# One more round of lag in the attention pipeline of a two-block fp32 kernel, with a third buffer for the probabilities

## The chip, the cores and the metric

The kernel runs on one NeuronCore of a Trainium2 chip. The metric is the device time of one execution in microseconds (us); lower is better. TensorE is called PE in the profile (PEld is its weight-load side), VectorE DVE, ScalarE ACT, GpSimd POOL and SyncE SP.

## What is computed

A sequence of 512 tokens of width 1024 goes through two layers of a first block and then two layers of a second block, all in float32. The parts of the reference that matter here are its attentions, each a masked softmax of scores times values, in blocks of 128 queries:

```python
def one_block(args):
    q_blk, blk = args
    s = jnp.einsum('bqhmd,bkhmd->bhmqk', q_blk, k).astype(jnp.float32) * scale
    ...
    s = jnp.where(mask, s, -jnp.inf)
    p = jax.nn.softmax(s, axis=-1).astype(v.dtype)
    return jnp.einsum('bhmqk,bkhd->bqhmd', p, v)
...
# first block, per layer
y_mem = memory_cross_attention(xq, mem_n, ...) @ w_cross_o[l]      # 4 heads, 256 memory rows
y_diff = diff_attention(dq, dk, dv, ...) @ w_diff_o[l]             # 8 heads, two maps each
y_mla = latent_attention(c_q, c_kv_kr, ...) @ w_mla_o[l]           # 8 heads of 96
merged = gates[:, :, 0] * y_diff + gates[:, :, 1] * y_mla + gates[:, :, 2] * y_mem
x = x + merged @ w_out[l]
# second block, per layer: dsa_mixer and nsa_mixer (4 heads each), a short convolution, a pooling
```

The second block's attentions are over compressed keys (31 of them), over selected and windowed keys, and over the top 128 keys of an index score.

## The kernel before, in words

Every engine has its own program, written out by hand in order, and they meet at counting semaphores. Projections (`project`, L377 and L379) take each weight slab of 128 rows through a ring of four slabs (SP issues the loads), POOL splits it into a high and a low part (L292, L295), and PE multiplies three combinations of parts, 12 matmuls of 512 columns a slab.

Attention is cut into units: one unit is a block of 128 queries for two heads (or the two maps of a head), with n keys. A unit takes six steps:

- `scores` (PE, L525, mask L530) into one of two pairs of PSUM banks (`u % 2`);
- `maximum` (DVE, L567);
- `exp` (ACT, L581) into one of two slots of `probs` (`u % 2`), with the row sums;
- `turn` (PE, L544, L546), the transposes of the probabilities into the one pair of banks 4 and 5;
- `copy` (ACT, L593) out of them into one of two slots of `probs_t`;
- `weight` (PE, L557), the products with the values, and `finish` (DVE, L1150 to L1167 and L1658 to L1677), the scaling by the row sums.

`attend` puts the PE steps into rounds: round i has scores of unit i, turn of unit i - 2, weight of unit i - 3, in this order. `steps` does the same for ACT (copy of i - 2, then exp of i) and DVE (maximum of i, finish of i - 3, and a piece of other work where `between` has one). Scores of unit i wait for exp of unit i - 2, since they share banks. There are 88 units a pass over both blocks: cross (8 units, n = 256), diff (32 units) and mla (16 units) in each layer of block one, and 32 in each layer of block two. In diff and mla the key counts follow one another as 128, 512, 256, 384.

Where attend has a `projection`, the rounds behind the last scores (the tail) are set in front of slabs 1, 2, ... of the next projection: `lat0` behind cross, `gate00` behind mla. Diff and block two have nothing between the tail's rounds. After the mla attention DVE squares and sums the diff outputs (L1248, L1250), scales them (L1254) and signals `outs_ready`, for which PE waits in front of the transposes `o_t0` and `o_t1` (L391); these follow `gate00`, and behind them stands the projection `gate01`.

Of the kernel before, what the change touches and what calls it, by code (L numbers as in the profile page):

```python
# [28 lines left out]
P = 128  # L29
# [3 lines left out]
W512 = 512  # L33
# [52 lines left out]
def program(nc, io, out):  # L86
    ctx = ExitStack()
    with ctx:
# [6 lines left out]
        m = {}  # L95
        for name, floats in (("arena", 80 * 256), ("outs", 32 * 256)):
# [9 lines left out]
            "probs": sb("probs", [P, 2, 2, W512]),  # L106
# [7 lines left out]
            "small": sb("small", [P, 2304]),  # L114
# [120 lines left out]
class Layer:  # L235
# [87 lines left out]
    def attend(self, pe, A, lo, hi, before_turns=None, projection=None):  # L323

        ahead, first = 0, self.done[-1 if len(self.done) % 2 else -2]
        if before_turns:
            ahead = 2  # L330

            def scores():
                self.emptied(pe, first)
                A.scores(lo)
                A.scores(lo + 1)

            self.project(pe, *before_turns, {4: scores})
        else:
            self.emptied(pe, first)
        parts = [(0, A.scores), (2, A.turn), (3, A.weight)]  # L340
        for i in range(lo, hi + 1):
            A.round(i, lo, hi, parts, ahead)
            if i == lo:
                self.emptied(pe, self.done[-1])
        for name in self.order.names[len(self.done):][:2]:
            self.first_wait[name] = (self.s["finished" if self.order.index(name) % 2 else "exped"], hi)
        tail = [lambda i=i: A.round(i, lo, hi, parts) for i in (hi + 1, hi + 2)]
        if projection:
            self.project(pe, *projection, {1 + k: f for k, f in enumerate(tail)})
        else:  # L350
            for f in tail:
                f()
# [140 lines left out]
class Attention:  # L493
# [39 lines left out]
    def turn(self, u):  # L533
        pe, a = self.nc.tensor, self.units[u]
        pe.wait_ge(self.s["exped"], u + 1)
        if u >= 1:
            pe.wait_ge(self.s["turned_copied"], u)
        for j in range(2):
            for kb in range(0, a["n"], P):
                src = self.m["probs"][:, u % 2, j, kb:min(kb + P, a["n"])]  # L540
                width = src.shape[1]
                dst = self.m["ps"][0:width, 4 + j, kb:kb + P]
                if width == P:
                    last = pe.transpose(dst, src, self.m["ident"][:])  # L544
                else:
                    last = pe.matmul(dst, src, self.m["ident"][:], start=True, stop=True)  # L546
        last.then_inc(self.s["turned"], 1)
# [27 lines left out]
    def exp(self, u):  # L575
        act, a = self.nc.scalar, self.units[u]
        act.wait_ge(self.s["maxed"], u + 1)
        if u >= 2:
            act.wait_ge(self.s["turned"], u - 1)
        for j in range(2):  # L580
            last = act.activation(self.m["probs"][:, u % 2, j, 0:a["n"]],  # L581
# [46 lines left out]
def block_one(nc, io, m, s, layer):  # L628
# [68 lines left out]
    gated, merging = (m[n][:].rearrange("p a b n -> p (a b) n") for n in ("probs", "probs_t"))  # L697
# [84 lines left out]
    with nc.Block() as block:  # L782
# [100 lines left out]
        def _(act):  # L883
# [82 lines left out]
            A.steps(0, U1, (2, A.copy), (0, A.exp), ahead=2)  # L966
# [20 lines left out]
            A.steps(U1, U2, (2, A.copy), (0, A.exp), between={prep_rounds[-2]: lambda: roots(st_both)})  # L987
# [4 lines left out]
            A.steps(U2, U3, (2, A.copy), (0, A.exp))  # L992
# [38 lines left out]
        def _(dve):  # L1031
# [139 lines left out]
            A.steps(0, U1, (0, A.maximum), (3, finish), ahead=2)  # L1171
# [69 lines left out]
            A.steps(U1, U2, (0, A.maximum), (3, finish), between=dict(zip(prep_rounds, pieces)))  # L1241
            A.steps(U2, U3, (0, A.maximum), (3, finish))
# [62 lines left out]
def block_two(nc, io, m, s, layer):  # L1305
# [67 lines left out]
    U = len(units)  # L1373
# [17 lines left out]
    with nc.Block() as block:  # L1391
# [70 lines left out]
        def _(act):  # L1462
# [57 lines left out]
            A.steps(0, U, (2, A.copy), (0, A.exp))  # L1520
# [3 lines left out]
        def _(dve):  # L1524
# [155 lines left out]
            A.steps(0, U, (0, A.maximum), (3, finish), between={2 + k: lambda k=k: piece(k) for k in range(len(ops))})  # L1680
# [9 lines left out]
            fresh = m["probs"][:].rearrange("p a b n -> p (a b) n")  # L1690
# [94 lines left out]
```

## Time and profile before

| what | value |
|---|---|
| median of 3 runs | 2975.85 us (2973.08 to 2976.11) |
| the profiled execution: time, span of its instructions | 2971.55 us, 2969.7 us |
| PE busy, share of the span | 2740.5 us, 92% |
| DVE, ACT, POOL busy | 1081.9, 746.6, 1868.5 us |
| mean granted clock of PE | 0.967 |

The busy time of PE has modelled ends, so a full row of PE means that it had work all along and not that it ran at its peak. The granted clock is 1.00 at 2.4 GHz and 0.50 at 1.2 GHz.

### The profile page before, as it was taken

Reading aid. Unit: us, or ns where it says so; the run is one execution under the profiler, and the core shown is the slowest. Engines: PE = TensorE matmul, PEld = TensorE weight load, DVE = VectorE, ACT = ScalarE, POOL = GpSimd, SP = SyncE. Lnnn points to the kernel's source line nnn. Section 1 sums busy time; section 2 is a strip of 40 time slices with the busy share of each in tenths; the row PEclk is TensorE's granted clock in tenths of the full one; section 3 lists DMA queues with packets and bytes.
Section 4 is the critical chain, followed back from the end, with each engine's and each line's share of the span. In section 5 each row is a group of like instructions: output and inputs, shape, how many; then the busy total and the mean of one; then the engine's idle time right before and its main releaser. Section 6 shows DMA issues by size and latency. Waiting matters only on the chain. (4 is left out here: it accounts for less than half of the span.)

```text
span 2969.7 us, 38883 instructions
## 1 busy us (share of the span) xinstructions
PE 2740.5 (92%) x14264; PEld 2252.2 (76%) x14268; DVE 1081.9 (36%) x1902; ACT 746.6 (25%) x1455; POOL 1868.5 (63%) x1562
## 2 busy tenths in 40 slices
PE   6898999999999997899999999999998998989997
PEld 4687777778888886678777778888887976778765
DVE  4354364211210113245183320310102486427773
ACT  3241464200220201331365110120111114212250
POOL 5547321788898995647420788898896772366604
PEclk9999999999999998999999999999998999999998
DMA  4322100233233333322100233223233430042202
GB/s 123 85 61 77 41 8 12 81 93 96 89 96 97 95 96 81 96 77 74 52 8 1 72 88 96 90 93 99 93 99 79 94 79 29 29 89 76 76 1 71
DMA packets 159285, 214.80 MB, mean 72 GB/s; under 512 B 51696, under 2 KB 69360, under 8 KB 159088
## 3 DMA queue, kind: packets, MB, share of 16 engines
q1 hardware_dynamic: 120336, 207.27, 24.1%
q10 hardware_dynamic: 38752, 4.95, 1.3%
q8 instruction: 118, 1.93, 0.3%
q14 instruction: 79, 0.65, 0.1%
HBM read 210.06 MB, written 2.10 MB: 71 GB/s over the span
## 5 line engine op out<-in xcount | busy, mean ns | idle before, releaser
L292 POOL TENSOR_TENSOR weight_parts<-weight_ring,zero 128x512 fp32r<-128x512 f32 (+3 forms) x736 | 791.2, 1075 | 775.8 <-PE ps L377 396.9
L295 POOL TENSOR_TENSOR weight_parts<-weight_ring,weight_parts 128x512 fp32r<-128x512 f32 (+4 forms) x804 | 1062.1, 1321 | 155.3 <-ACT weight_parts L303 97.0
L379 PE MATMUL ps<-h_feature_major_high,weight_parts 128*128 128x512 f32 x2304 | 584.8, 394 | 13.1 <-ACT arena L1486 5.3
L379 PEld LDWEIGHTS ps<-h_feature_major_high,weight_parts 128*128 128x128 f32 x2304 | 431.0, 189 | 117.1 <-POOL weight_parts L292 10.0
L377 PE MATMUL ps<-weight_parts,h_feature_major_high 128*128 128x512 f32 (+3 forms) x1920 | 438.7, 369 | 39.1 <-DVE h_feature_major_low L1687 9.1
L377 PEld LDWEIGHTS ps<-weight_parts,h_feature_major_high 128*128 128x128 f32 x1920 | 344.3, 193 | 94.4 <-issue 18.8
L379 PE MATMUL ps<-h_feature_major_low,weight_parts 128*128 128x512 f32 x1152 | 310.0, 391 | 0.0
L377 PE MATMUL ps<-weight_parts,ut_high 128*128 128x512 f32 x1024 | 254.7, 390 | 0.0
L379 PEld LDWEIGHTS ps<-h_feature_major_low,weight_parts 128*128 128x128 f32 x1152 | 217.5, 189 | 45.8
L377 PE MATMUL ps<-weight_parts,h_feature_major_low 128*128 128x512 f32 (+3 forms) x960 | 234.7, 368 | 0.0
L377 PEld LDWEIGHTS ps<-weight_parts,ut_high 128*128 128x128 f32 x1024 | 191.6, 188 | 42.2 <-POOL weight_parts L295 1.7
L567 DVE TENSOR_REDUCE negmax<-ps 128x2 f32<-128x512 f32 (+4 forms) x176 | 132.7, 754 | 240.1 <-ACT arena L985 113.9
L557 PE MATMUL ps<-arena,probs_key_major 128*128 128x128 f32 (+1 forms) x1632 | 216.4, 279 | 0.0
L525 PE MATMUL ps<-arena 64*128 64x512 f32 (+9 forms) x704 | 169.7, 480 | 42.5 <-ACT probs L581 23.8
L557 PEld LDWEIGHTS ps<-arena,probs_key_major 128*128 128x128 f32 (+1 forms) x1632 | 198.5, 194 | 6.5 <-issue 6.0
L581 ACT ACTIVATE probs<-ps,negmax 128x256 f32<-128x256 f32 (+4 forms) x352 | 172.7, 499 | 97.7 <-DVE negmax L567 87.1
L377 PEld LDWEIGHTS ps<-weight_parts,h_feature_major_low 128*128 128x128 f32 x960 | 176.0, 194 | 24.1
L1295 DVE TENSOR_TENSOR ut_low<-outs,ut_high 128x2048 fp32r<-128x2048 f32 x16 | 45.1, 2816 | 319.6 <-ACT ut_high L1027 319.6
L593 ACT ACTIVATE probs_key_major<-ps 128x512 f32<-128x512 f32 (+4 forms) x176 | 116.6, 662 | 122.5 <-PE ps L544 113.9
L1023 ACT ACTIVATE outs<-ps 128x2048 f32<-128x2048 f32 x16 | 30.1, 1883 | 429.7 <-PE ps L379 429.7
L377 PE MATMUL ps<-weight_parts,ut_low 128*128 128x512 f32 x512 | 136.9, 390 | 0.0
L525 PEld LDWEIGHTS ps<-arena 64*128 64x128 f32 (+2 forms) x704 | 76.9, 200 | 73.5 <-ACT probs L581 33.1
(245 smaller groups left out, 2848.8 us busy)
## 6 DMA issues: line engine op xcount, KB each, us to landing
weight_ring<-in_w_in SPq DMA_DIRECT2D x272, 256.0 KB, 2.7
weight_ring<-in_w_mlp SPq DMA_DIRECT2D x256, 256.0 KB, 2.7
weight_ring<-in_w_out SPq DMA_DIRECT2D x64, 256.0 KB, 2.6
weight_ring<-in_w_mem_kv SPq DMA_DIRECT2D x32, 256.0 KB, 2.9
weight_ring<-in_w_diff_o SPq DMA_DIRECT2D x32, 256.0 KB, 2.6
weight_ring<-in_w_in SPq DMA_DIRECT2D x32, 170.0 KB, 2.7
weight_ring<-in_w_in SPq DMA_DIRECT2D x32, 168.0 KB, 2.2
weight_ring<-in_w_in SPq DMA_DIRECT2D x32, 163.0 KB, 2.2
```

Source lines behind the costliest of these rows:

```text
L292: self.nc.gpsimd.tensor_tensor(high, raw, self.m["zero"][:].broadcast_to([P, raw.shape[1]]), ALU.add).then_inc(self.s["slab_high"], 1)
L295: self.nc.gpsimd.tensor_tensor(low, raw, high.bitcast(F32), ALU.subtract).then_inc(self.s["slab_split"], 1)
L377: last = self.nc.tensor.matmul(banks[:, t, 0:width], h[:, cut], w, **ends)
L379: last = self.nc.tensor.matmul(banks[:, t, :], w[:, cut], h, **ends)
L525: last = pe.matmul(bank[:, 0:a["n"]], a["q"][j], a["k"][j], start=True, stop=a["mask"] is None)
L557: last = pe.matmul(self.m["ps"][:, 6 + u % 2, j * P:(j + 1) * P], self.m["probs_t"][0:rows, u % 2, j, kb * P:(kb + 1) * P], a["v"][j](kb), ...
L567: last = dve.tensor_reduce(out, self.m["ps"][:, 2 * (u % 2):2 * (u % 2) + 2, 0:a["n"]], AX.X, ALU.max, negate=True)
L581: last = act.activation(self.m["probs"][:, u % 2, j, 0:a["n"]], self.m["ps"][:, 2 * (u % 2) + j, 0:a["n"]], ACT.Exp, bias=self.m["negmax"] ...
L593: act.activation(self.m["probs_t"][0:rows, u % 2, :, 0:width], self.m["ps"][0:rows, 4:6, 0:width], ACT.Copy).then_inc(self.s["turned_copie ...
L1023: a.activation(r, L.banks(f"up{f}{j}"), ACT.Relu)
L1295: v.tensor_tensor(ut[1][:, 4 * j:4 * j + 4, :], rect[(f * ups + j) % 2], ut[0][:, 4 * j:4 * j + 4, :].bitcast(F32), ALU.subtract).then_inc ...
```

## The change

The transposes move from two to three rounds behind the scores, the value products and the finish from three to four, and `probs` gets a third slot, so that exp of unit u waits for the transposes of unit u - 3 instead of u - 2. The tail of each attend has one more round. The scratch `small` is shortened from 2304 to 2128 floats to make room. The PSUM banks of the scores stay two pairs, and `probs_t` keeps two slots.

```diff
-            "probs": sb("probs", [P, 2, 2, W512]),
+            "probs": sb("probs", [P, 3, 2, W512]),
...
-            "small": sb("small", [P, 2304]),
+            "small": sb("small", [P, 2128]),
...
-        parts = [(0, A.scores), (2, A.turn), (3, A.weight)]
+        parts = [(0, A.scores), (3, A.turn), (4, A.weight)]
...
-        tail = [lambda i=i: A.round(i, lo, hi, parts) for i in (hi + 1, hi + 2)]
+        tail = [lambda i=i: A.round(i, lo, hi, parts) for i in (hi + 1, hi + 2, hi + 3)]
...
-                src = self.m["probs"][:, u % 2, j, kb:min(kb + P, a["n"])]
+                src = self.m["probs"][:, u % 3, j, kb:min(kb + P, a["n"])]
...
         act.wait_ge(self.s["maxed"], u + 1)
-        if u >= 2:
-            act.wait_ge(self.s["turned"], u - 1)
+        if u >= 3:
+            act.wait_ge(self.s["turned"], u - 2)
         for j in range(2):
-            last = act.activation(self.m["probs"][:, u % 2, j, 0:a["n"]],
+            last = act.activation(self.m["probs"][:, u % 3, j, 0:a["n"]],
...
-            A.steps(0, U1, (2, A.copy), (0, A.exp), ahead=2)
+            A.steps(0, U1, (3, A.copy), (0, A.exp), ahead=2)
...
-            A.steps(0, U1, (0, A.maximum), (3, finish), ahead=2)
+            A.steps(0, U1, (0, A.maximum), (4, finish), ahead=2)
...
```

The other calls of `steps` change in the same way, and three views of `probs` as scratch take its first two slots.

On PE, at the start of the diff attention (first layer), the rounds of units 3 to 5 stood so (L525 and L530 scores and mask, L544 transposes, L557 value products):

```order
246 L525 MATMUL ps<-arena 128x384 x2
247 L530 MATMUL ps<-causal,ident 128x128 x2
248 L544 MATMUL ps<-ident,probs 128x128 x8
249 L557 MATMUL ps<-arena,probs_key_major 128x128 x2
250 L525 MATMUL ps<-arena 128x128 x2
251 L530 MATMUL ps<-causal,ident 128x128 x2
252 L544 MATMUL ps<-ident,probs 128x128 x4
253 L557 MATMUL ps<-arena,probs_key_major 128x128 x8
254 L525 MATMUL ps<-arena 128x512 x2
255 L530 MATMUL ps<-causal,ident 128x128 x2
256 L544 MATMUL ps<-ident,probs 128x128 x6
257 L557 MATMUL ps<-arena,probs_key_major 128x128 x4
```

The same rounds in the changed kernel:

```order
245 L525 MATMUL ps<-arena 128x384 x2
246 L530 MATMUL ps<-causal,ident 128x128 x2
247 L544 MATMUL ps<-ident,probs 128x128 x2
248 L525 MATMUL ps<-arena 128x128 x2
249 L530 MATMUL ps<-causal,ident 128x128 x2
250 L544 MATMUL ps<-ident,probs 128x128 x8
251 L557 MATMUL ps<-arena,probs_key_major 128x128 x2
252 L525 MATMUL ps<-arena 128x512 x2
253 L530 MATMUL ps<-causal,ident 128x128 x2
254 L544 MATMUL ps<-ident,probs 128x128 x4
255 L557 MATMUL ps<-arena,probs_key_major 128x128 x8
```

The transposes of each unit stand one round later and so behind the scores of another unit: the 4 transposes of a 256-key unit stood behind the short scores of a 128-key unit, and stand now behind the long ones of a 512-key unit.

On PE, where the mla attention ends and `gate00` begins (L379), the order was:

```order
427 L557 MATMUL ps<-arena,probs_key_major 128x128 x8
428 L379 MATMUL ps<-h_feature_major_high,weight_parts 128x512 x4
429 L379 MATMUL ps<-h_feature_major_low,weight_parts 128x512 x4
430 L379 MATMUL ps<-h_feature_major_high,weight_parts 128x512 x4
431 L544 MATMUL ps<-ident,probs 128x128 x6
432 L557 MATMUL ps<-arena,probs_key_major 128x128 x4
433 L379 MATMUL ps<-h_feature_major_high,weight_parts 128x512 x4
434 L379 MATMUL ps<-h_feature_major_low,weight_parts 128x512 x4
435 L379 MATMUL ps<-h_feature_major_high,weight_parts 128x512 x4
436 L557 MATMUL ps<-arena,probs_key_major 128x128 x6
```

In the changed kernel the same place reads, from the end of slab 0 on:

```order
429 L544 MATMUL ps<-ident,probs 128x128 x4
430 L557 MATMUL ps<-arena,probs_key_major 128x128 x8
431 L379 MATMUL ps<-h_feature_major_high,weight_parts 128x512 x4
432 L379 MATMUL ps<-h_feature_major_low,weight_parts 128x512 x4
433 L379 MATMUL ps<-h_feature_major_high,weight_parts 128x512 x4
434 L544 MATMUL ps<-ident,probs 128x128 x6
435 L557 MATMUL ps<-arena,probs_key_major 128x128 x4
436 L379 MATMUL ps<-h_feature_major_high,weight_parts 128x512 x4
437 L379 MATMUL ps<-h_feature_major_low,weight_parts 128x512 x4
438 L379 MATMUL ps<-h_feature_major_high,weight_parts 128x512 x4
439 L557 MATMUL ps<-arena,probs_key_major 128x128 x6
```

The last value products stood behind two slabs of `gate00` and now stand behind three, and one more unit's transposes and value products moved from in front of `gate00` into it.

## Rows read from the trace of the kernel before

**Rows 1.** The page: span, and busy time of the engines
```profile
span 2969.7 us, 38883 instructions
...
PE 2740.5 (92%) x14264; PEld 2252.2 (76%) x14268; DVE 1081.9 (36%) x1902; ACT 746.6 (25%) x1455; POOL 1868.5 (63%) x1562
```

**Rows 2.** Instructions of line 544 (turn): what its engine's idle time waited for
```profile
  ACT probs_key_major L593: 8.3, 21
  ACT probs L581: 1.6, 2
```

**Rows 3.** Instructions of line 557 (weight): what its engine's idle time waited for
```profile
  ACT probs_key_major L593: 0.4, 2
```

**Rows 4.** The waits: who waited for whom, total us, times, longest us
```profile
PEld ps L525 <- ACT probs L581: 33.1, 44, 1.5
```

**Rows 5.** Windows: stretch, us, each engine busy (instructions), PEclk granted, DMA share, GB/s
```profile
336.00:432.00 96.00, 86.19 (x659) 65.25 (x659) 73.00 (x169) 60.85 (x172) 16.02 (x12) 0.98 0.03 7
448.00:500.00 52.00, 48.57 (x308) 38.04 (x307) 21.24 (x55) 28.86 (x83) 0.00 (x0) 0.90 0.00 1
451.60:461.60 10.00, 9.66 (x30) 6.10 (x28) 2.87 (x3) 2.81 (x10) 0.00 (x0) 0.50 0.00 0
...
528.30:532.00 3.70, 3.66 (x32) 3.42 (x32) 1.03 (x2) 1.75 (x4) 3.54 (x4) 1.00 0.10 11
1662.00:1665.90 3.90, 3.89 (x24) 3.90 (x25) 0.55 (x1) 1.27 (x3) 3.74 (x4) 0.65 0.13 16
2480.00:2535.00 55.00, 49.75 (x379) 36.76 (x378) 47.36 (x125) 30.63 (x98) 0.00 (x0) 1.00 0.01 1
```

**Rows 6.** Timeline (start us, us, engine, line, op, [idle before]): DVE, block two
```profile
2497.21 0.15 DVE L1662 RECIPROCAL recip<-rowsum 128x2 f32<-128x2 f32 x1
...
2498.41 1.22 DVE L1626 TENSOR_TENSOR arena<-arena,small 64x1024 f32<-64x1024 f32 x1
```

**Rows 7.** Timeline, end of mla, gate00 and the transposes behind it, first layer
```profile
498.10 0.63 PE L544 MATMUL ps<-ident,probs 128*128 128x128 f32 x4 [0.76 <-ACT probs_key_major L593]
...
500.27 1.17 PE L379 MATMUL ps<-h_feature_major_high,weight_parts 128*128 128x512 f32 x4
...
507.41 1.50 PE L557 MATMUL ps<-arena,probs_key_major 128*128 128x128 f32 x12
...
512.40 1.07 PE L379 MATMUL ps<-h_feature_major_low,weight_parts 128*128 128x512 f32 x4
...
515.12 1.07 PE L379 MATMUL ps<-h_feature_major_low,weight_parts 128*128 128x512 f32 x4
...
528.25 3.71 PE L391 MATMUL ps<-ident,outs 128*128 128x128 f32 x32 [2.63 <-DVE outs L1254]
...
533.80 1.17 PE L379 MATMUL ps<-h_feature_major_high,weight_parts 128*128 128x512 f32 x4 [1.84 <-issue]
```

**Rows 8.** Timeline, PE at the same place in the second layer
```profile
1662.01 5.38 PE L391 MATMUL ps<-ident,outs 128*128 128x128 f32 x32 [2.63 <-DVE outs L1254]
1668.18 1.16 PE L379 MATMUL ps<-h_feature_major_high,weight_parts 128*128 128x512 f32 x4 [0.80 <-issue]
```

**Rows 9.** Timeline, DVE between cross attention and its work on the latent
```profile
250.66 0.77 DVE L1047 SCALAR_TENSOR_TENSOR outs<-arena 128x384 f32<-128x384 f32 x1 [17.09 <-ACT arena L910]
```

**Rows 10.** Timeline of PE, in the diff attention of the first layer
```profile
382.92 0.63 PE L544 MATMUL ps<-ident,probs 128*128 128x128 f32 x4 [0.30 <-ACT probs_key_major L593]
383.28 1.87 PEld L557 LDWEIGHTS ps<-arena,probs_key_major 128*128 128x128 f32 x16
...
386.04 1.13 PE L525 MATMUL ps<-arena 64*128 64x512 f32 x4 [0.71 <-ACT probs L581]
...
392.68 0.86 PEld L544 LDWEIGHTS ps<-ident,probs 128*128 128x128 f32 x8
```

**Rows 11.** Timeline, PE at the end of block two's attention, first layer
```profile
2555.11 1.07 PE L544 MATMUL ps<-ident,probs 128*128 128x128 f32 x8 [0.63 <-ACT probs_key_major L593]
```

More of the change, by code:

```diff
@@ L696, in block_one @@
     gates = [view(arena, 16384 + 2048 * k, 4, SEQ) for k in range(2)]
-    gated, merging = (m[n][:].rearrange("p a b n -> p (a b) n") for n in ("probs", "probs_t"))
+    gated, merging = (m[n][:, 0:2].rearrange("p a b n -> p (a b) n") for n in ("probs", "probs_t"))
     od = view(outs, 0, TT, D)
@@ L986, in _ @@
                 last.then_inc(emptied, 1)
-            A.steps(U1, U2, (2, A.copy), (0, A.exp), between={prep_rounds[-2]: lambda: roots(st_both)})
+            A.steps(U1, U2, (3, A.copy), (0, A.exp), between={prep_rounds[-2]: lambda: roots(st_both)})
             for k in range(2):
@@ L991, in _ @@
                 scaled(f"m_t{2 + k}", [(kmt[0:MQK, 4 * k + h, :], h, MQK, SEQ, mkg[0:MQK]) for h in range(4)])
-            A.steps(U2, U3, (2, A.copy), (0, A.exp))
+            A.steps(U2, U3, (3, A.copy), (0, A.exp))
             roots(st_o)
@@ L1240, in _ @@
             L.emptied(dve, "kvb1")
-            A.steps(U1, U2, (0, A.maximum), (3, finish), between=dict(zip(prep_rounds, pieces)))
-            A.steps(U2, U3, (0, A.maximum), (3, finish))
+            A.steps(U1, U2, (0, A.maximum), (4, finish), between=dict(zip(prep_rounds, pieces)))
+            A.steps(U2, U3, (0, A.maximum), (4, finish))
             v.drain()
@@ L1519, in _ @@
             empty("cmp_t", [(kcmpt, L.banks("cmp_t")[:, 0, 0:NCMP], ACT.Copy, 1.0)])
-            A.steps(0, U, (2, A.copy), (0, A.exp))
+            A.steps(0, U, (3, A.copy), (0, A.exp))
             L.square_right(act, 1, junk)
@@ L1678, in finish @@
                 last.then_inc(s["finished"], 1)
-            A.steps(0, U, (0, A.maximum), (3, finish), between={2 + k: lambda k=k: piece(k) for k in range(len(ops))})
+            A.steps(0, U, (0, A.maximum), (4, finish), between={2 + k: lambda k=k: piece(k) for k in range(len(ops))})
             def mix_in(src, at, chunks):
@@ L1689, in _ @@
             full(dve, "mix_t")
-            fresh = m["probs"][:].rearrange("p a b n -> p (a b) n")
+            fresh = m["probs"][:, 0:2].rearrange("p a b n -> p (a b) n")
             v.tensor_tensor(fresh, L.banks("mix_t"), fm[:, 0:4, :], ALU.mult)
```

## The prediction

> **What bounds the kernel now.** I read the page first. PE is busy for 2740.5 of 2969.7 us [rows 1], so the kernel is bound by PE's work and by the places where PE stands idle. The change adds and removes no matmul, so it can act only on idle time and on the clock. Next I read the waits for the pairs that the lag touches. A later turn can relieve two of them: turn waiting for its own unit's exp, 1.6 us in 2 instances [rows 2], and weight waiting for the copy, 0.4 us in 2 [rows 3]. The whole relief it is made for is 2.0 us of 2970. The large wait is another: scores wait 33.1 us, 44 times, for the exp of the unit two before, because the scores have two pairs of banks [rows 4]. That distance stays two, and the third slot of probabilities gives them no bank. The slot itself is only what the longer lag needs: exp would otherwise wait for transposes that stand a round later.
>
> Then I read the stages by windows [rows 5]. In diff PE has 86.19 busy us of 96, in mla 48.57 of 52: mostly bound by PE, where idle can hardly shrink. In block two's attention, from 2480 to 2535, DVE is busy for 47.36 of 55 us and its steps follow one another (the finish of a unit runs from 2497.21 until other work begins at 2498.41 [rows 6]): bound by DVE. The total of DVE's work does not change either.
>
> Last I read what stands behind the attention. In mla's layer PE finishes `gate00` and then waits 2.63 us for the scaled outputs, in both layers [rows 7, 8]. So the DVE chain from the last finish to `outs_ready` is not hidden now. Whatever delays the last value products delays the kernel.
>
> **The change part by part.** All terms are for one layer; there are two of each.
>
> *Cross.* Its tail lies in `lat0` and grows by one slab. Key counts are all equal, so nothing is re-paired. DVE ends later by about a slab, but it stands idle for 17.09 us between its work on the queries and keys and the latent's [rows 9], so this costs nothing; without that cover it would be a slab, up to 2.7 us.
>
> *Diff.* One gain and one loss. The gain: once in four rounds, the transposes of a 256-key unit wait some 0.3 us for the copy of a 512-key unit (382.92 [rows 10]); 8.3 us in 21 instances over the kernel [rows 2]. Now the scores of a 512-key unit, 1.13 us instead of a 128-key unit's, stand between them, so that wait goes: at most 7 times 0.3 = 2.1 us. The loss: while PE waits for exp (0.71 at 386.04 [rows 10]), it has done less than before, by one unit's transposes and value products. After the last such wait PE is the bound and owes that unit. For the largest unit this is 0.86 + 1.87 = 2.7 us [rows 10]; for the mean unit, with 2.5 blocks of keys against 4, 1.7 us. The first rounds also have one less turn to fill the wait for the first exps. Between -2.1 and +2.7, neither end nearer by any row, I take a little above the middle: +0.5.
>
> *mla and the outputs.* Before `gate00` the last transposes wait 0.76 us for the copy of the 512-key unit [rows 7]. They move into `gate00` behind a slab and this wait goes: -0.7. The last value products now stand behind three slabs instead of two. One slab takes 2.72 us (512.40 to 515.12 [rows 7]). From the value products at 507.41 to the transposes at 528.25 DVE's chain takes 20.8 us and I leave it as it is. So `outs_ready` comes 2.7 - 0.7 = 2.0 us later, while PE arrives 0.7 earlier: its wait grows from 2.63 to about 5.3 us, and the kernel loses +2.0. Bounds: 1.3 (two waits of 0.7 saved) to 2.7 (none).
>
> *Block two.* One unit's finish, 1.2 us (2497.21 to 2498.41 [rows 6]), leaves the stretch that DVE bounds and falls behind it, where DVE has time: -1.2. The turn's wait for its exp stands at this stage's start, half of the 1.6 us a layer [rows 2]: -0.8. The tail has one more round in which transposes and copy take turns, where a single wait was 0.63 [rows 11]: +0.4. Sum -1.6, bounds -2.0 and +0.6 (only the tail's loss).
>
> *The clock.* The same wait of 2.63 us leaves the clock at 1.00 in the first layer and brings it to 0.65 on the mean in the second, where the transposes take 5.38 instead of 3.71 us [rows 5, 7, 8]. A wait of 5.3 us should bring it down in both. What is behind needs the first 16 of the 32 transposes: half of 3.71, 1.85 us, at half the clock 1.85 more; I take 1.6 in the first layer. In the second layer `gate01` starts 6.17 us after the transposes begin against 5.55 in the first, so 0.6 is paid already; the clock falling earlier adds 0.7. Together +2.3 for both layers, between 0 and 3.1. The Trainium skill, TensorE: Matmul & The Clock Gate, "Why this matters for your kernels", says to leave no longer idle gaps between bursts of matmuls, as the clock falls to half after them. [...]
>
> **Sum.** 2 x (0 + 0.5 + 2.0 - 1.6) + 2.3 = +4.1 us. Against the profiled execution, 2971.55, this is 2975.7; that run lies 4.3 us below the median of the runs, so against the median 2975.85 I predict 2980. This is 0.14% slower. A difference of 0.2%, 6 us, is about what can be told from no change here.
>
> **The rivals.**
>
> *Half the clock lasts longer (slower).* At mla's start PE runs 10 us at 0.50, busy for 9.66 of them [rows 5], and block two has a like stretch. With one round more of scores alone, PE's work there is thinner. If each of the four stretches is a third longer, 3.4 us, half is lost: 4 x 1.7 = 6.8. With the forecast's 4.1 this is +11, 2987. It decides from about 2 us of loss on. Against it: a change of the mix could as well end the stretches sooner. The Trainium skill, the same page, "Part 4: PE-mode transpose", says that transposes do not count as busy for the clock. By that the 32 transposes behind the longer wait would not bring it back, and `gate01` would start slow as well. In the second layer the mean clock over the transposes is 0.65 and not 0.50 throughout [rows 5], which is no proof either way.
>
> *No change.* The re-pairing gives all of its gain (diff -2.1, block two -2.0) and the outputs' delay is 2.0: 2 x (-2.1 + 2.0 - 2.0) + 0 to 2.3 = -4.2 to -1.9, about 2973. Speaks for it: each bound is a row; against: the debt of one unit in diff.
>
> *Faster.* The lag changes how ACT's rounds are filled. In blocks of 128 keys, copy plus exp were 3, 7, 3, 7 in four rounds and are now 5, 6, 5, 4; PE's rounds go from 7, 9, 6, 8 to 6, 10, 7, 7. Evener rounds on ACT could let exp come sooner, and the 33.1 us of waits [rows 4] shrink. The losses above are 2 x 2.0 + 2.3 = 6.3 us, so it needs 12.3 us of 33.1 to be told as faster; with half, -16.5, it gives 2966. Against it: in block two, and in diff's first rounds, exp waits for a maximum that DVE's other work holds up (DVE busy 47.36 of 55 and 73.00 of 96 us [rows 5]), not for ACT.
>
> **How the numbers follow.** Forecast +4.1, own range 0 to +8 (2976 to 2984): 0.52, of which 0.14 lies above +6. Longer half clock: 0.18. No change: 0.18. Faster: 0.12. So faster 0.12, same 0.38 + 0.18 = 0.56, slower 0.14 + 0.18 = 0.32. The range that leaves out 2 in 10 reaches from 2969, between the faster case and no change, to 2988, just above the longer half clock.
>
> **What would show it.** In the trace after: turn's wait for exp gone, and few waits of L544 for L593 between the rounds; the waits of L525 for L581 still at some 30 us or more; the wait of the transposes L391 for L1254 at about 5 us in both layers, and the clock below 1.00 behind it in both; diff's stage as long as before within 2 us; block two's attention 1 to 2 us shorter. I am wrong if L525's waits fall by a third or more, if the wait for `outs_ready` stays near 2.6, or if the stretches at 0.50 change in length.

## The result, and the profile after

| | kernel before | changed kernel |
|---|---|---|
| median, beside each other on one chip | 2974.80 us (2969.24 to 2980.51, 20 runs) | 2983.08 us (2975.43 to 2990.96, 20 runs) |
| ratio, 95% interval | | 1.0026 [1.0018, 1.0034] |
| span of the profiled execution | 2969.7 us | 2981.4 us |
| mean granted clock of PE | 0.967 | 0.962 |

The changed kernel is 0.26% slower, about 7.7 us. The time lies in the forecast's range (2969 to 2988) and 3 us above its value of 2980. Taken as a difference, the growth of 7.7 us is nearly twice the forecast +4.1; that the two times lie closer comes from the median of the kernel before, which is 1 us lower here than the one that the forecast started from. Of the three cases I had held "within 0.2%" the likeliest; it became "slower", with the lower end of its interval (1.0018) just short of that line. Block two's term came out with the wrong sign, and those of mla and diff at another size. Line numbers of the changed kernel are those of before. In the experiments they are 1 to 7 higher, so L544 of the profile can be L545 or L548 there.

The page of the changed kernel answers to [rows 1]: no work was added, and PE is still busy for 92%.
```profile
span 2981.4 us, 38883 instructions
...
PE 2748.3 (92%) x14268; PEld 2261.8 (76%) x14268; DVE 1086.7 (36%) x1902; ACT 751.8 (25%) x1455; POOL 1870.4 (63%) x1562
```

The waits of the changed kernel, who waited for whom with the total, the times and the longest, answer to [rows 4]:
```profile
PEld ps L525 <- ACT probs L581: 31.8, 34, 2.2
```
The sum of the scores' waits stayed (33.1 before), but they are 34 in place of 44 and the longest has grown from 1.5 to 2.2 us. What L544 waits for answers to [rows 2]:
```profile
  ACT probs_key_major L593: 5.3, 8
  ACT probs L581: 1.3, 2
```
The waits for the copy fell from 21 to 8, by 3.0 us, and the two for exp hardly moved (1.6 to 1.3). One of these two stands here, first in the kernel before and then in the changed one; the other is at the same place of the second layer:
```profile
2555.08 0.86 PEld L544 LDWEIGHTS ps<-ident,probs 128*128 128x128 f32 x8 [0.79 <-ACT probs L581]
2562.27 0.64 PEld L544 LDWEIGHTS ps<-ident,probs 128*128 128x128 f32 x6 [0.65 <-ACT probs L581]
```
Both stand in the tail of block two's attention, behind its last scores.

PE's timeline at the outputs, first and second layer, answers to [rows 7, 8]:
```profile
531.20 5.44 PE L391 MATMUL ps<-ident,outs 128*128 128x128 f32 x32 [5.42 <-DVE outs L1254]
...
1670.00 6.05 PE L391 MATMUL ps<-ident,outs 128*128 128x128 f32 x32 [5.42 <-DVE outs L1254]
```
The wait for the outputs doubled in both layers, from 2.63 to 5.42 us, as forecast.

Last, the stages by windows, in the columns of [rows 5]: diff, then mla up to the first output transposes, then from these to those of `o_t2`, then the same three of the second layer, then block two's attention twice.
```profile
337.43:437.73 100.30, 89.79 (x674) 69.23 (x673) 74.29 (x172) 62.42 (x172) 16.03 (x12) 0.95 0.02 6
451.60:531.20 79.60, 70.48 (x435) 57.27 (x434) 40.56 (x75) 36.06 (x91) 23.09 (x15) 0.96 0.09 24
531.20:582.09 50.89, 49.07 (x225) 41.30 (x226) 5.36 (x8) 7.16 (x12) 37.09 (x32) 0.96 0.27 78
1474.26:1574.65 100.39, 89.77 (x673) 69.37 (x673) 74.39 (x172) 62.46 (x172) 16.02 (x12) 0.95 0.02 6
1588.52:1670.00 81.48, 73.35 (x436) 59.35 (x434) 40.66 (x75) 36.17 (x91) 23.08 (x15) 0.92 0.09 24
1670.00:1720.89 50.89, 49.68 (x225) 41.91 (x226) 5.36 (x8) 7.22 (x12) 37.08 (x32) 0.95 0.27 78
2475.67:2569.08 93.41, 87.43 (x616) 65.17 (x617) 63.63 (x175) 50.95 (x161) 0.42 (x1) 0.91 0.01 4
2816.80:2910.24 93.44, 87.55 (x616) 65.25 (x617) 63.58 (x175) 50.94 (x161) 0.42 (x1) 0.91 0.01 4
```
The same eight stretches of the kernel before, cut at the same instructions, are these:
```profile
336.04:433.94 97.90, 88.08 (x673) 66.98 (x673) 73.99 (x172) 61.30 (x172) 16.02 (x12) 0.98 0.02 7
447.81:528.25 80.44, 74.39 (x436) 59.12 (x434) 40.57 (x75) 34.89 (x91) 20.80 (x13) 0.94 0.08 21
528.25:577.44 49.19, 47.35 (x224) 39.59 (x225) 5.36 (x8) 7.15 (x12) 39.32 (x34) 1.00 0.30 86
1469.40:1567.47 98.07, 88.09 (x673) 67.01 (x673) 74.01 (x172) 61.30 (x172) 16.02 (x12) 0.98 0.02 7
1581.34:1662.01 80.67, 74.41 (x436) 58.93 (x434) 40.59 (x75) 34.88 (x91) 20.81 (x13) 0.94 0.08 21
1662.01:1711.81 49.80, 49.01 (x225) 41.26 (x226) 5.45 (x8) 7.26 (x12) 39.32 (x34) 0.97 0.30 85
2467.34:2560.05 92.71, 84.70 (x614) 62.97 (x617) 63.32 (x175) 50.82 (x161) 0.41 (x1) 0.94 0.01 4
2805.70:2898.22 92.52, 84.62 (x614) 63.00 (x617) 63.30 (x175) 50.84 (x161) 0.42 (x1) 0.94 0.02 4
```
Read the length, PE's busy time and the clock of each pair. The eight stretches hold 9.1 of the 11.7 us between the two spans. Diff grew by 2.4 and 2.3 us, the stretch behind the outputs by 1.7 and 1.1, and block two by 0.7 and 0.9. Mla shrank by 0.8 in one layer and grew by 0.8 in the other. In every stretch that grew, the clock fell. Mla's second layer grew by idle time too: 8.1 us against 6.3, while PE's busy time fell by 1.1. Its first layer is short by the clock: near its start this is at 0.50 for 3.4 us (459.7 to 463.1), where before it was for 10 us [rows 5]. With the long distance mla alone took 81.5 us in both layers (`mla_only` below), so 79.60 is not its usual length. The remaining 2.6 us lie outside these eight, 1.3 of them ahead of the first attention, where the change does nothing, and such stretches vary by as much among the kernels below.

### The profile page after: what moved, and what is told of

Its sections match the earlier page's. It is cut to its first block and busy times, and to the rows that moved or that the text cites. A ratio compares the mean times of both kernels' runs of the same rounds, so it can differ in the third digit from the quotient of the medians.

```text
span 2981.4 us, 38883 instructions
## 1 busy us (share of the span) xinstructions
PE 2748.3 (92%) x14268; PEld 2261.8 (76%) x14268; DVE 1086.7 (36%) x1902; ACT 751.8 (25%) x1455; POOL 1870.4 (63%) x1562
## 5 line engine op out<-in xcount | busy, mean ns | idle before, releaser
L379 PE MATMUL ps<-h_feature_major_high,weight_parts 128*128 128x512 f32 x2304 | 585.3, 394 | 13.9 <-ACT arena L1486 5.8
L379 PEld LDWEIGHTS ps<-h_feature_major_high,weight_parts 128*128 128x128 f32 x2304 | 431.1, 189 | 117.4 <-ACT arena L1486 9.4
L379 PE MATMUL ps<-h_feature_major_low,weight_parts 128*128 128x512 f32 x1152 | 310.0, 391 | 0.0
L379 PEld LDWEIGHTS ps<-h_feature_major_low,weight_parts 128*128 128x128 f32 x1152 | 217.3, 189 | 46.1
L557 PE MATMUL ps<-arena,probs_key_major 128*128 128x128 f32 (+1 forms) x1632 | 220.5, 282 | 0.0
L525 PE MATMUL ps<-arena 64*128 64x512 f32 (+9 forms) x704 | 172.2, 491 | 43.1 <-ACT probs L581 24.6
L557 PEld LDWEIGHTS ps<-arena,probs_key_major 128*128 128x128 f32 (+1 forms) x1632 | 202.5, 197 | 6.7 <-issue 6.1
L525 PEld LDWEIGHTS ps<-arena 64*128 64x128 f32 (+2 forms) x704 | 79.2, 207 | 73.7 <-ACT probs L581 31.8
```

Of the source, the lines that this page charges most:

```text
L379: last = self.nc.tensor.matmul(banks[:, t, :], w[:, cut], h, **ends)
L525: last = pe.matmul(bank[:, 0:a["n"]], a["q"][j], a["k"][j], start=True, stop=a["mask"] is None)
L557: last = pe.matmul(self.m["ps"][:, 6 + u % 2, j * P:(j + 1) * P], self.m["probs_t"][0:rows, u % 2, j, kb * P:(kb + 1) * P], a["v"][j](kb), ...
```

## Experiments: one stage at a time

All four have the third slot and the smaller `small`. The distances of transposes and value products can be set for each stage; short is 2 and 3 rounds, long is 3 and 4. The kernel before took 2974.43 us beside them. The code shows `slot_only`, with all four distances short; the other three set one of them to 3.
```diff
+LAG = dict(cross=2, diff=2, mla=2, two=2)
...
-        parts = [(0, A.scores), (3, A.turn), (4, A.weight)]
+        parts = [(0, A.scores), (lag, A.turn), (lag + 1, A.weight)]
...
-        tail = [... for i in (hi + 1, hi + 2, hi + 3)]
+        tail = [... for i in range(hi + 1, hi + lag + 1)]
```

**The slot alone (`slot_only`).** 

> The third slot of probabilities and the shortened scratch alone, with the transposes two and the value products three rounds behind as before (exp waits for the transposes of unit u - 3). Theory (the lag costs, the slot does nothing, since scores and exp keep their two pairs of banks): ratio to before 1.000, within 0.001. Rival (the moved buffers or the third slot cost by themselves): 1.002 to 1.003.

Measured: 2973.34 us, 1.0001 [0.9989, 1.0013]. Its windows for diff in the two layers:
```profile
335.28:433.33 98.05, 88.10 (x673) 67.01 (x673) 74.00 (x172) 61.37 (x172) 16.03 (x12) 0.98 0.02 7
1467.50:1566.43 98.93, 89.23 (x672) 67.82 (x671) 74.11 (x172) 61.28 (x172) 16.02 (x12) 0.97 0.03 6
```
The slot costs and brings nothing that can be told (its interval reaches from -3 to +4 us). The two layers run the same program and differ by 0.9 us, with the clock at 0.98 and 0.97: this much a stage moves by itself.

**Long in block two alone (`two_only`).** 

> Three slots everywhere, the longer lag in block two alone. From the trace of the changed kernel, which stands 0.7 and 0.9 us later at the end of this stage and 1.6 us later behind its first layer, theory: +3 us, ratio 1.001; PE's waits for exp gathered in a few of over 1 us, and a stretch at half the clock in the middle of the stage. By the prediction's term (-1.6 a layer): -3 us, ratio 0.999, no such stretch.

Measured: 2978.02 us, 1.0004 [0.9995, 1.0013]. Its two stages of block two, and a stretch in the first:
```profile
2474.20:2567.60 93.40, 87.37 (x616) 65.12 (x617) 63.65 (x175) 50.95 (x161) 0.42 (x1) 0.91 0.01 4
2519.80:2526.60 6.80, 6.75 (x25) 4.04 (x26) 5.57 (x15) 2.73 (x11) 0.00 (x0) 0.50 0.01 4
2815.68:2908.16 92.48, 87.21 (x616) 64.91 (x617) 63.45 (x175) 50.82 (x161) 0.42 (x1) 0.91 0.01 4
```
PE's idle time, length less busy time, is 6.0 and 5.3 us, against 8.0 and 7.9 in the kernel before: it fell by 2.0 and 2.6 us where I had forecast a stage shorter by 1.6. The stage is no shorter for it: `slot_only`, with short distances, takes 93.59 and 92.33 us. The clock is 0.91 and not 0.94, and PE's busy time grew by 2.6. The interval holds no change as well as the theory's 1.001; it leaves out the 0.999 of the prediction's term.

**Long in diff alone (`diff_only`).** 

> Three slots everywhere, the longer lag in the diff attention alone. Theory by the trace of the changed kernel (the stage 2.4 us longer in each layer): +4.7 us, ratio 1.0016, waits of PE for exp of 1.8 us and more, and stretches at half the clock inside the stage. By the prediction's term (+0.5 a layer): +1 us, ratio 1.0003. Rival (the gain of re-pairing alone, the clock falls being chance): below 1.000.

Measured: 2974.81 us, 1.0001 [0.9992, 1.0010]. Its windows for diff:
```profile
336.94:435.46 98.52, 87.79 (x673) 67.46 (x673) 74.19 (x172) 62.31 (x172) 16.02 (x12) 0.97 0.02 6
1471.40:1571.84 100.44, 89.80 (x674) 69.43 (x675) 74.35 (x172) 62.47 (x172) 16.03 (x12) 0.95 0.02 6
```
The same stage of the same program takes 98.5 in one layer and 100.4 us in the other. Idle is alike (10.7 and 10.6 us); busy time and clock differ. The total leaves out the 1.0016 that the changed kernel's trace had suggested. So the long distance costs 0.6 to 0.9 us by its waits, and up to 2 us more when the clock falls inside the stage. The gain that I had forecast, the transposes' waits for the copy, is not there. These are the transposes in diff's first layer, in the kernel before and in the changed one (busy us, mean ns, idle us ahead of them):
```profile
L544 PE MATMUL ps<-ident,probs 128*128 128x128 f32 x160 | 23.2, 276 | 2.1 <-ACT probs_key_major L593 1.6
L544 PE MATMUL ps<-ident,probs 128*128 128x128 f32 x160 | 24.0, 282 | 2.0 <-ACT probs_key_major L593 2.0
```
The waits for the copy went from 1.6 to 2.0 us. In mla they went from 1.4 us to nothing (`mla_tail2_only` below), and that is where most of the 3.0 us was saved.

**Long in mla alone (`mla_only`).** 

> Three slots everywhere, the longer lag in the mla attention and its tail in the gate projection alone. Theory by the prediction's terms (+2.0 a layer for the outputs that come later, +2.3 for the clock behind the longer wait): +6 us, ratio 1.002; the wait of the transposes for the scaled outputs 4.5 to 5.3 us in both layers. By the trace of the changed kernel the net was +0.9 and +1.9 us: +3 us, ratio 1.001. Rival (the outputs are hidden): 1.000 and a wait of 2.6 us.

Measured: 2978.81 us, 1.0010 [1.0001, 1.0019]; the only one of the four whose interval leaves out 1. Mla in the first layer took 81.52 us, as in the second; the stretch behind the outputs took 50.90 and 50.89:
```profile
450.22:531.74 81.52, 73.38 (x436) 58.60 (x434) 40.67 (x75) 36.17 (x91) 23.09 (x15) 0.92 0.09 24
```
With short distances the first of these is 80.65 us in both layers and the second 49.7 and 49.8. So mla itself loses 0.9 a layer, and what is behind it 1.1. Twice their sum is 4 us: half of the change's 7.7.

## Experiments: the place of the last value products, and the clock

The kernel before took 2973.08 us beside the next four; each is the changed kernel with one more edit.

**Mla's first two closing rounds ahead of one slab (`mla_tail2`).** The long distance stays, but the last value products stand behind two slabs again.
```diff
+        if projection and projection[0] == "gate00" and lag == 3:
+            a, b, c = tail
+            tail = [lambda: (a(), b()), c]
```


> The long round everywhere, but in mla's tail both of the first two closing rounds stand ahead of the first output slab, so that the last value products stand behind two slabs as they did before. My theory (the wait for the outputs grew because the last unit's value products stand one slab later): TensorE's wait ahead of the first output transposes falls from 5.42 us to about 2.7 to 3.5 us, each mla stage is 1 to 2.7 us shorter, and the first tail's stretch o_t0 to o_t2 lies nearer 49.8 than 50.9 us; together 3 to 6 us below the changed kernel, 1.001 of before or less. Rival (the wait only moves, because ScalarE and VectorE are still behind by the longer round): the waits appear inside the slab or at the earlier closing round, and the time stays that of the changed kernel, 1.0026.

Measured: 2972.93 us, 0.9997 [0.9988, 1.0006]. The whole loss of the change is gone. PE's timeline at the outputs:
```profile
528.69 5.38 PE L395 MATMUL ps<-ident,outs 128*128 128x128 f32 x32 [2.62 <-DVE outs L1258]
```
And the window of mla in the second layer; the first took 78.78 us too:
```profile
1586.73:1665.51 78.78, 73.46 (x435) 59.23 (x433) 40.68 (x75) 36.17 (x91) 20.77 (x13) 0.94 0.08 21
```
Mla takes 2.7 us less than in the changed kernel's second layer, which is a slab, and 1.9 less than with short distances. The wait is back at 2.62. The stretch behind the outputs took 50.2 and 50.4 us, between the two values expected. Two slabs and these two stretches make 6.7 us; the ratios of the two kernels stand 0.0029, or 8.6 us, apart, with an uncertainty of some 3.6. The profiled execution, 2978.13 us, was 5.2 us above its kernel's median, so its stages in diff and block two can be longer than usual.

**Extra products in the wait for the outputs (`keep_outs`).** Their results are not read.
```diff
+                        L.emptied(pe, L.order.names[L.order.index(name) - 2])
+                        pe.wait_ge(s["finished"], U3)
+                        for _ in range(16):
+                            nc.tensor.matmul(L.banks(name)[:, 0, :], ht[0][:, 0, 0:P], ht[0][:, 1, :], start=True, stop=True)
                         pe.wait_ge(s["outs_ready"], 1)
```


> The changed kernel with sixteen extra 512-column products, whose result nobody reads, in the 5.4 us in which TensorE waits for the last outputs of mla. Theory that the long wait costs more than itself, by the stretch at 0.50 of the clock behind it: the stretch at 0.50 behind the first output transposes is gone or at most 3.4 us long, o_t0 to o_t2 takes 49.2 to 49.8 us in both layers and not 50.9, the mla stage itself stays at 81.5 us; 2 to 3.5 us below the changed kernel, about 1.0016 of before. Rival (the fall of the clock has another cause, such as the small products behind it): no change, or the extra products come late and cost up to 1 us a layer.

Measured: 2984.92 us (5 runs), 1.0040 [1.0026, 1.0055]. PE's timeline at the outputs:
```profile
528.43 3.79 PE L852 MATMUL ps<-h_feature_major_high 128*128 128x512 f32 x16
534.04 3.71 PE L392 MATMUL ps<-ident,outs 128*128 128x128 f32 x32 [1.82 <-DVE outs L1259]
```
And the window of the stretch behind in the first layer; the second took 49.18 us, at a clock of 1.00 too:
```profile
534.04:583.24 49.20, 47.36 (x224) 39.58 (x225) 5.36 (x8) 7.15 (x12) 37.06 (x32) 1.00 0.27 81
```
In place, the theory holds: PE is busy for 3.8 of the 5.4 us, the clock stays at 1.00, and the stretch takes 49.2 in place of 50.9 us in both layers. The whole did not get measurably faster, and the 1.0016 that I expected lies outside the interval. Its profiled span is 2981.4 us, that of the changed kernel. The 3.4 us gained here are missing elsewhere: 1.9 us in mla's first layer (81.50 against 79.60, where the changed kernel's profile was the short one), 0.7 in diff's first, and 2.3 just ahead of block two (186.7 against 184.4). Whether preventing a fall of the clock in one place pays in the whole is not shown: one profile of each kernel and five runs don't settle 3 us.

**Extra products in diff's waits (`keep_diff`).** Before the scores of four units, 29 products of 256 columns a layer, behind a wait for `finished` that keeps their bank free.
```diff
+    for u, keep in ((3, 4), (4, 3), (11, 10), (17, 12)):
+        units[U1 + u]["keep"] = keep
...
+        if a.get("keep"):
+            pe.wait_ge(self.s["finished"], u - 5)
+        for _ in range(a.get("keep", 0)):
+            pe.matmul(self.m["ps"][:, 6 + u % 2, 256:512], self.m["ht"][0][:, 0, 0:P], self.m["ht"][0][:, 1, 0:256], start=True, stop=True)
```


> The changed kernel with extra 256-column products, whose result nobody reads, ahead of the scores of four diff units (4, 3, 10 and 12 of them), where TensorE now waits 0.7 to 2.0 us for the exponentials. Theory that diff's loss is the clock that falls behind its gathered waits: the stretches at 0.50 inside diff (three of 3.4 us in each layer) go, and the stage takes about 98.5 us and not 100.3 in both layers; 3 to 4 us below the changed kernel, 1.0013 of before. Rival (the loss is in the waits themselves, or the extra products push the scores late): the stage stays at 100 us or more.

Measured: 2987.78 us (5 runs), 1.0042 [1.0028, 1.0056]. Ten of the extra products in PE's timeline, and what they waited for:
```profile
369.40 1.46 PE L523 MATMUL ps<-h_feature_major_high 128*128 128x256 f32 x10 [1.30 <-DVE outs L1165]
```
The windows of diff in the first layer (101.28 us in the second), and of block two's first layer, which the edit leaves alone:
```profile
338.71:440.16 101.45, 92.13 (x702) 71.03 (x702) 74.45 (x172) 62.56 (x172) 16.02 (x12) 0.97 0.02 6
2481.51:2578.52 97.01, 93.29 (x616) 68.93 (x617) 64.05 (x175) 51.20 (x161) 0.41 (x1) 0.84 0.01 4
```
The stage came out as the rival said, over 100 us, but by the experiment's construction. The wait for the bank (1.30 us) took the place of the wait for exp, so the products came late. The clock rose to 0.97 from 0.95, but PE's busy time grew by 2.3. It neither shows nor refutes the theory for diff. Block two at a clock of 0.84 shows how far a stage can move that nobody edited.

**Diff's query blocks in another order (`order_after`).**
```diff
-        for i in (0, 3, 1, 2):
+        for i in (3, 2, 0, 1):
```


> The changed kernel with each diff head's query blocks in the order of 512, 384, 128 and 256 keys in place of 128, 512, 256 and 384, so that a large unit's exponentials no longer stand behind another large one's transposes in the same place. Theory that the gathered waits come from the sizes' pattern against the distance of three rounds: the waits for exponentials in diff spread or shrink, the stage takes 98 to 99 us, 2 to 4 us in all below the changed kernel, 1.001 to 1.002 of before. Rival (ScalarE's work for the sum of four units is what TensorE waits for, whatever the order): the waits only change place and the stage stays at 100 us, 1.0026.

Measured: 2980.11 us, 1.0022 [1.0012, 1.0032]. The window of diff in the first layer; the second took 98.69 us:
```profile
337.53:436.23 98.70, 88.47 (x673) 68.39 (x673) 74.05 (x172) 62.05 (x172) 16.01 (x12) 0.97 0.03 6
```
And the longest wait in PE's timeline there:
```profile
369.46 0.70 PE L526 MATMUL ps<-arena 64*128 64x256 f32 x4 [2.11 <-ACT probs L582]
```
The stage is 1.6 us shorter, as expected, but not for the reason given: the waits neither spread nor shrank (one is 2.11 us; idle is 10.2 against 10.5 us). The clock fell twice inside the stage and not three times. The total moved by less than the intervals are wide.

## Experiments: is the slab enough, and is there a faster kernel

The kernel before took 2976.11 us beside these.

**Short distances, the last value products one slab later (`tail_late`).**
```diff
-            self.project(pe, *projection, {1 + k: f for k, f in enumerate(tail)})
+            self.project(pe, *projection, {1: tail[0], 3: tail[1]} if projection[0] == "gate00" else {1 + k: f for k, f in enumerate(tail)})
```


> The short distances everywhere (two and three rounds, with the third slot), and in mla's tail the second closing round, with the last value products, stands ahead of the third slab in place of the second, one slab later than in the kernel before. Theory (the change's loss in mla is the slab on which the last value products stand, not the longer distance): TensorE's wait ahead of the first output transposes grows from 2.63 to 5.4 us, mla takes about 83.4 us where short distances gave 80.65, o_t0 to o_t2 takes 50.9 us, and the whole is 6 to 9 us above the kernel before, 1.0025. Rival (the wait also needs the longer distance, since ScalarE and VectorE are then behind by a round): the wait stays under 4 us and the time within 3 us of before.

Measured: 2982.99 us, 1.0030 [1.0019, 1.0040]: the changed kernel's loss without its distance. PE's timeline at the outputs:
```profile
532.77 6.26 PE L392 MATMUL ps<-ident,outs 128*128 128x128 f32 x32 [5.42 <-DVE outs L1255]
```
The windows of mla and of the stretch behind, in the second layer (83.11 and 50.90 us in the first):
```profile
1585.85:1669.12 83.27, 74.29 (x435) 59.01 (x433) 40.57 (x75) 34.89 (x91) 23.09 (x15) 0.93 0.09 23
1669.12:1720.01 50.89, 50.03 (x225) 42.27 (x225) 5.45 (x8) 7.27 (x12) 37.05 (x32) 0.95 0.27 78
```
The wait is 5.42 us, mla 2.5 and 2.6 us longer than 80.65, and the stretch behind 50.9. The total is 7 us above the kernel before, as expected. The rival (that the wait needs the longer distance too) has fallen.

**Long in mla alone, with its first two closing rounds ahead of one slab (`mla_tail2_only`).** The edits of `mla_only` and `mla_tail2` together. 

> The long round in mla alone, with its two first closing rounds ahead of the first slab, and short distances elsewhere. Theory: mla takes 78.8 us and not 80.65 in both layers, the wait for the outputs stays at 2.6 us, diff takes 98.0 to 98.9 us as with short distances; in all 3 to 4 us below the kernel before, ratio 0.9987. Rival (what a stage gains is lost in how the clock falls elsewhere): the stage lengths come out so and the ratio stays within 0.0007 of 1.

Measured: 2972.62 us, 0.9991 [0.9981, 1.0001]. The window of mla in the second layer; the first took 78.80 us:
```profile
1581.06:1659.85 78.79, 73.45 (x435) 58.81 (x433) 40.69 (x75) 36.17 (x91) 20.76 (x13) 0.93 0.08 21
```
And the transposes of the probabilities in that window, by line: busy us, mean ns, idle us ahead of them.
```profile
L548 PE MATMUL ps<-ident,probs 128*128 128x128 f32 x80 | 12.0, 283 | 0.0
```
Here the longer distance does what it can do. With short distances the same row has 12.5 us, and 1.4 us of idle time ahead of it for the copies; these are gone, and the waits for exp grew by 0.5. The stage is 1.9 us shorter, of which 1.0 is seen so in waits and 0.5 in the transposes' own time. The rest I can't place.

**All long, both repairs (`tail2_order_after`).** The edits of `mla_tail2` and `order_after` together. 

> The changed kernel with both repairs: the two first closing rounds of mla ahead of the first slab, and diff's query blocks in the order 512, 384, 128 and 256 keys. Theory (the two effects are independent and add up): mla 78.8 us, diff 98.7 us in both layers, 3 us below the kernel with the first repair alone, ratio to before 0.9987. Rival (the clock's stretches move and eat the order's gain): 0.9997 as with the first repair alone.

Measured: 2972.39 us, 0.9991 [0.9979, 1.0002]. Diff in both layers, and block two in the first:
```profile
336.26:436.10 99.84, 89.94 (x673) 69.65 (x673) 74.48 (x172) 62.28 (x172) 16.02 (x12) 0.95 0.02 6
1469.08:1566.89 97.81, 86.93 (x673) 67.31 (x673) 74.01 (x172) 61.90 (x172) 16.03 (x12) 0.98 0.03 7
2465.12:2560.89 95.77, 91.60 (x614) 68.03 (x617) 63.93 (x175) 51.16 (x161) 0.42 (x1) 0.86 0.01 4
```
Diff came out at 99.8 and 97.8 us for one program, and block two at 95.8 with a clock of 0.86 where the changed kernel had 93.4 and 0.91. The order's gain can't be told from this: 0.9991 is within the interval of the kernel without it, 0.9997 [0.9988, 1.0006].

**Long in mla alone, and another order in diff (`tail2_order_before`).**
```diff
-        for i in (0, 3, 1, 2):
+        for i in (2, 3, 1, 0):
```


> Long distance in mla alone with the first two closing rounds ahead of the first slab, short distances elsewhere, and diff's query blocks in the order 384, 512, 256 and 128 keys. Theory (the waits for the exponentials in diff hang on which sizes stand three rounds apart, for the short distance too): the waits in the short pipeline, 5.0 us summed over the stage before, shrink and diff takes 97.0 to 97.8 us; ratio 0.9983. Rival (in the short pipeline the order changes nothing, or for the worse since the last unit of a head is the smallest): diff takes 98 to 99 us, ratio 0.9987 or above.

Measured: 2971.77 us, 0.9988 [0.9977, 0.9999]. Diff took 98.65 us in both layers, no less than with the old order (97.97 and 98.83): the theory about the order falls, and its rival holds. The scores' waits for exp did not shrink either: 7.4 us in diff's first layer, against 5.9 with the old order.

## Why the prediction came out as it did

**The reading of the waits: right for the scores, wrong for the turn.** The scores' waits for exp kept their sum (33.1 to 31.8 us), and the copies' waits shrank by 3.0 us. What I did not read is how they are dealt out: the sum stood, the number fell, the longest grew. The turn's wait for its own exp I had put at the start of block two's stage and said it would be gone. It stands in the tail, where no later scores stand between, and 1.3 of its 1.6 us stayed. PEld's wait at 2555.08 and PE's at 2555.11 [rows 11] are one wait of the same transposes, put down to exp in one row and to the copy in the other; I had counted it as a gain of 0.8 and again under the tail's loss of 0.4.

**mla and the outputs: mechanism right, +2.0 a layer, measured +0.9.** The value products one slab later are worth 2.5 to 2.7 us (81.52 in `mla_only` against 78.79 with the long distance, 83.11 and 83.27 against 80.65 with the short), and the wait for the outputs grew to 5.42 us against a forecast of 5.3. The term that was off is the gain ahead of it: I counted one wait for a copy, 0.7 us, and the long distance takes 1.9 out of the stage, of which waits are 1.0.

**The clock behind that wait: right, +2.3 for both layers.** Measured 1.7 + 1.1 = 2.8 us against the profile before, and 2.2 against `slot_only` (49.73 and 49.84). The extra products, which hold the clock at 1.00 and bring the stretch to 49.2, show it to be the clock. The slab with what hangs on it is worth as much as the whole result: undoing it alone moves the ratio from 1.0026 to 0.9997, and making it alone moves 1.0001 to 1.0030. It is not the only term, though. With the long distance in mla alone, undoing it moves 1.0010 to 0.9991. By stages it costs some 3.7 us a layer, and the long distance in mla gives 1.9 back; the rest of the 7.7 us, some 4, is left to diff, block two and cross.

**Block two: wrong, -1.6 forecast, +0.8 measured.** Against `slot_only` it is +0.5. The step that failed is that a shorter wait of PE makes a shorter stage. The idle time did fall, by 2.0 us (8.0 to 6.0). But PE's busy time grew by 2.7 us, with a new stretch at half the clock inside the stage. The longest wait in PE's timeline there:
```profile
2519.22 0.41 PE L525 MATMUL ps<-arena 64*128 64x31 f32 x4 [1.51 <-ACT probs L581]
```
Behind it, from 2521.30 to 2528.10, the clock is 0.50; the second layer has the like at 2862.7, and `two_only` the one shown above. DVE, which I had called the bound of this stage, is busy for 63.6 of its 93.4 us, PE for 87.4.

**Diff: +0.5 forecast, +2.4 measured.** By its waits alone it is +0.6 (98.5 in `diff_only`'s first layer against 97.9). That this is near +0.5 is luck: +0.5 was the middle of a wide range, and the gain in it, the copy's waits, did not come (1.6 to 2.0 us). The rest is the clock again. The changed kernel's waits there are 1.80 and 2.02 us where before had 1.18 and less, and behind the first of them the clock is down. The timeline, and then the window:
```profile
369.47 0.92 PE L525 MATMUL ps<-arena 64*128 64x384 f32 x4 [1.80 <-ACT probs L581]
```
```profile
370.90:374.30 3.40, 3.40 (x20) 2.95 (x19) 3.09 (x6) 1.24 (x6) 0.00 (x0) 0.51 0.00 0
```
That gathered waits bring the clock down is argued from their order in the trace and not shown: the experiment for it missed. A fall also does not follow each such wait: `order_after` has one of 2.11 us ahead of 369.46 and ran on at full clock behind it, and so did the changed kernel behind its own 2.02 us, ahead of 388.21.

**The rivals.** The longer half clock (+11 us) named the right effect in the wrong place. It was to lengthen the stretches at the starts of mla and block two; those kept their 10 us or lost some, and new ones appeared in the middle. Its 6.8 us happen to be near the 6.3 us by which diff and block two grew. Here the prediction's own sign of being wrong came up: stretches at 0.50 did change in length. "Faster" failed as its own test said: the scores' waits did not fall by a third.

**What stays open.** Diff, mla and block two each vary by 1 to 4 us with where the clock's falls land. Two pairs of kernels price the long distance in cross, diff and block two together. With the outputs repaired it costs 0.9997 - 0.9991, 0.0006 with about 0.0013 of uncertainty, so between -2 and +6 us. Without the repair it costs 1.0026 - 1.0010, 0.0016 with about 0.0012, so between 1 and 8 us. The profiles before and after show 6.3 us of growth in diff and block two; how much of it a typical execution has is not settled. The runs of single stages, added up, give 1.0013 and not 1.0026, with an uncertainty larger than that difference. Cross alone was not run.

**A faster kernel.** The four kernels with the long distance in mla and the last value products back behind two slabs are at 0.9997, 0.9991, 0.9991 and 0.9988. Only the last one's interval (up to 0.9999) leaves out 1. It is the best seen, by some 3.5 us, about half of what I called measurable. As the lowest of twelve, and with its siblings' intervals around it, it isn't shown to be faster.

## What to carry to other kernels

When a pipeline is made longer, look first at what its tail delays: here one slab of the next projection, put ahead of the last value products, cost more than all that the distance could win in mla, and moving it back took a few lines. A PE wait is not its length only: ask whether the clock stays up behind it. For an edit that gathers waits, look at the longest as well as at their sum; that the longest decides was not shown here. Find each wait's place in time before you count it: the same wait counted at a stage's start and in its tail gave two terms here. Where the clock decides, compare a stage in every layer and in several kernels that share it before a microsecond is given a cause.

## What the runs showed of the hardware

A long wait ahead of the output transposes always cost the clock: in all ten layers with 5.42 us (two each of the changed kernel, `mla_only`, `tail_late`, `order_after` and `keep_diff`) the stretch behind took 50.7 to 50.9 us. With 2.6 us, in the sixteen layers of eight kernels, it took 49.2 us in five, at a clock of 1.00, and 49.7 to 50.8 in eleven, at 0.97, in the same program too (49.19 and 49.80 before). The Trainium skill, TensorE: Matmul & The Clock Gate, "Why this matters for your kernels", advises against long gaps, with a bound that lies between these two. The traces agree for 5.4 us; the waits of 2.6 us are below the bound, and in eleven of sixteen layers the clock fell all the same.

Transposes alone brought the clock back. Behind the wait of 5.42 us, in the changed kernel's first layer, PE runs only transposes, from 531.20 to 536.64:
```profile
531.20:534.80 3.60, 3.60 (x17) 3.60 (x18) 0.00 (x0) 0.00 (x0) 2.11 (x2) 0.50 0.10 10
534.80:536.60 1.80, 1.80 (x17) 1.60 (x15) 0.97 (x2) 1.69 (x3) 0.00 (x0) 1.00 0.37 126
```
The kernel issues them as `nc.tensor.transpose` (L391). The Trainium skill, the same page, "Part 4: PE-mode transpose", says that transposes don't count as busy for the clock in the same way. This trace differs, and the measurement decides.
